# Transposing DMAs for seven heads' outputs and ScalarE's own x*sigmoid(x) in the first layer of a two-layer trunk

## The reference, cut to what matters

```python
proj = x @ w_in
xm, z, o_pre = proj[..., :E], proj[..., E:2 * E], proj[..., 2 * E:3 * E]      # E = 2048, 8 heads of 256
xc = jax.nn.silu(_causal_dwconv(xm, conv_w, conv_b))                          # 4 taps
q, k = xc @ w_q * DK ** -0.5, xc @ w_k                                        # by head
v = xm @ w_v
h = _mlstm_chunkwise(q, k, v, i_pre, log_sigmoid(f_pre))                      # 8 chunks of 128 tokens
hn = (h - mean(h)) * rsqrt(var(h) + eps) * norm_g                             # over a head's 256 channels
hb = sigmoid(o_pre) * hn + skip * xc
branch = (hb * jax.nn.silu(z)) @ w_out
x = layer_norm(alpha * x + branch)
```

## Time and profile before

| what | value |
|---|---|
| median of 3 runs (lowest to highest) | 1388.66 us (1387.12 to 1392.43) |
| the profiled execution: its time, its span | 1388.29 us, 1386.5 us |
| TensorE busy | 1374.8 us, 99% of the span |
| VectorE busy | 1155.4 us, 83% |
| ScalarE busy | 754.4 us, 54% |
| GpSimd busy | 147.5 us, 11% |
| chain that ended last | TensorE 94%, VectorE 3%, ScalarE 1% |

### The profile page before, as it was taken

The page is one execution under the profiler, slowest core; times in us unless marked ns, Lnnn a source line. Parts: engine busy times, 40 slices in busy tenths (PEclk is TensorE's granted clock), DMA queues, the critical chain, the costliest instruction groups (busy, mean ns, idle before and its releaser), DMA issues.

```text
span 1386.5 us, 19098 instructions
## 1 busy us (share of the span) xinstructions
PE 1374.8 (99%) x6602; PEld 1150.8 (83%) x6602; DVE 1155.4 (83%) x1891; ACT 754.4 (54%) x1318; POOL 147.5 (11%) x246
## 2 busy tenths in 40 slices
PE   9999999999999999999999999999999999999997
PEld 7888888888888888888888888888888888888886
DVE  6989899898998989899874446797888888889976
ACT  5775766657576674757733436564333333336340
POOL 1001011010201101010000001001111111100021
PEclk9999999999999999999999999999999999999999
DMA  6115344262534426245497767434666555699651
GB/s 235 49 39 145 97 123 112 72 182 54 140 96 118 118 76 172 65 137 180 138 334 244 221 190 226 129 118 112 168 159 165 156 135 157 180 298 324 215 198 76
DMA packets 103809, 213.44 MB, mean 154 GB/s; under 512 B 11010, under 2 KB 27906, under 8 KB 102562
## 3 DMA queue, kind: packets, MB, share of 16 engines
q1 hardware_dynamic: 90914, 178.66, 38.7%
q0 software_dynamic: 12800, 33.56, 13.0%
HBM read 170.11 MB, written 75.63 MB: 177 GB/s over the span
## 4 chain that ended last, share of the span: by engine, by line
PE 94%; DVE 3%; ACT 1%; DMA 1%; issue 1%; POOL 0%; DVEq 0%; SPq 0%; ACTq 0%; POOLq 0%
PE wide L2935 20%; PE wide L2937 20%; PE wide L2936 20%; PE ps_state L2935 3%; PE ps_state L2937 3%; PE ps_state L2936 3%; PE ps_inter L2936 2%; PE ps_inter L2935 2%; PE ps_inter L2937 2%; PE ps_intra L3114 2%; PE ps_intra L2937 2%; PE ps_intra L2935 2%; PE ps_s L2935 2%; PE ps_s L2936 2%; PE ps_s L2937 2%; PE ps_intra L2936 2%
## 5 line engine op out<-in xcount | busy, mean ns | idle before, releaser
L2936 PE MATMUL wide<-xa,inb 128*128 128x512 f32 x576 | 224.7, 390 | 0.0
L2935 PE MATMUL wide<-xb,inb 128*128 128x512 f32 x472 | 189.5, 402 | 0.7 <-DVE inb L1941 0.5
L2937 PE MATMUL wide<-xb,inb 128*128 128x512 f32 x472 | 184.3, 391 | 0.0
L2936 PEld LDWEIGHTS wide<-xa,inb 128*128 128x128 f32 x576 | 108.4, 188 | 20.2
L2936 PE MATMUL wide<-xa,blk 128*128 128x512 f32 x320 | 124.5, 389 | 0.0
L2937 PEld LDWEIGHTS wide<-xb,inb 128*128 128x128 f32 x472 | 88.6, 188 | 19.2
L2935 PEld LDWEIGHTS wide<-xb,inb 128*128 128x128 f32 x472 | 88.8, 188 | 18.5 <-issue 0.8
L2935 PE MATMUL wide<-xb,blk 128*128 128x512 f32 x256 | 99.7, 389 | 0.0
L2937 PE MATMUL wide<-xb,blk 128*128 128x512 f32 x256 | 99.6, 389 | 0.0
L1860 ACT ACTIVATE wy<-wy_raw 128x1024 fp32r<-128x1024 f32 x56 | 59.4, 1062 | 61.0 <-DMA wy_raw<-y_block 60.7
L2935 PE MATMUL wide<-xa,inb 128*128 128x512 f32 x208 | 83.2, 400 | 0.7 <-DVE inb L1941 0.7
(11 more groups left out here) (439 smaller groups left out, 3951.3 us busy)
## 6 DMA issues: line engine op xcount, KB each, us to landing
in_raw<-in_w_in SPq DMA_DIRECT2D x45, 512.0 KB, 4.2
wy_raw<-y_block SPq DMA_DIRECT2D x56, 256.0 KB, 4.2
mw_raw<-h_block SPq DMA_DIRECT2D x53, 256.0 KB, 3.3
m_sum<-in_w_out POOLq DMA_DIRECT2D x48, 256.0 KB, 4.3
h_block<-f_buf SPq DMA_DIRECT2D x48, 256.0 KB, 3.5
w_sum<-in_pool_w_out POOLq DMA_DIRECT2D x48, 256.0 KB, 4.3
a_raw<-in_pool_w_z SPq DMA_DIRECT2D x16, 512.0 KB, 3.7
a_raw<-folded SPq DMA_DIRECT2D x16, 512.0 KB, 4.6
```

What stands on the lines that cost most here:

```text
L2935: pe.matmul(dst, a[0], b[0], start=first, stop=False, skip_group_check=more)
L2936: pe.matmul(dst, a[0], b[1], start=False, stop=False, skip_group_check=more)
L2937: return pe.matmul(dst, a[1], b[0], start=False, stop=last, skip_group_check=more)
```

## The change

The outputs of heads 0 to 6 are no longer turned by TensorE (`turn_head` is gone; the last head's `turn` stays). In its place, for each half f of a head's chunks: `part_turn` (ScalarE, two copies 128x1024) takes the float32 numbers apart into their two 16-bit halves in `apart`; `move_turned` (SyncE) turns each of the two with a DMA transpose, 128 by 8 blocks of 128; `join_turn` (ScalarE, two copies) joins the halves again in `joined`, from which `y_turned` reads. On all eight heads the activation function Silu takes the place of tanh and VectorE's product: `silu_z` and `silu_conv` write in place, `gate_out_z` and `gate_conv` are gone, and the factors that undid the missing halves are dropped in `scale_columns`. Silu lies in another activation table than Exp and Tanh, so a table is loaded before the first `silu_z` and again by the preload of Exp. The queues are written in another order around this.

```diff
+            def move_turned(h, f):
+
+                sp.wait_ge(h_apart, 2 * h + f + 1)
+                if f:
+                    sp.wait_ge(h_moved, 64 * h + 32)
+                for part in range(2):
+                    sp.dma_start_transpose(turned_at(f, part), apart[:, f, part, :]).then_inc(h_moved, 16)
...
             for h in range(1, HEADS):
                 load_in(3 * h + 1, 0)
                 load_in(3 * h + 1, 1)
+                move_turned(h - 1, 0)
                 load_qkv(h)
                 load_in(3 * h + 2, 0)
                 load_rows(h)
-                store_h(h - 1, 1, 2)
+                move_turned(h - 1, 1)
                 load_in(3 * h + 2, 1)
-                store_h(h - 1, 5, 3, 7)
+                store_h(h - 1, 1, 2, 5, 3, 7)
...
+            def silu_z(h, n):
+
+                ready, (j, m) = ((in_c11, (0, 0)), (in_c22, (1, 1)), (in_c21, (1, 0)), (in_c12, (0, 1)))[n]
+                act.wait_ge(ready, 3 * h + 2)
+                act.activation(z_buf[:, j, half(m)], z_buf[:, j, half(m)], ACT.Silu).then_inc(z_made[n // 2], 1)
...
-            def tanh_conv(h, j):
+            def silu_conv(h, j):
                 act.wait_ge(conv_ready, 2 * h + 2 - j)
+                act.activation(xc_at(h, j), xc_at(h, j), ACT.Silu).then_inc(xc_ready, 1)
...
+            def part_turn(h, f, part):
+
+                act.wait_ge(hn_ready, 2 * h + f + 1)
+                act.wait_ge(s_full, NC * (h + 1))
+                ins = act.activation(apart[:, f, part, :].rearrange("p (c d) -> p c d", d=DV),
+                                     num[:, 4 * f:4 * f + 4, 0:DV].bitcast(U16).rearrange("p c (d b) -> p c d b", b=2)[:, :, :, part], ACT.Copy)
+                if part:
+                    ins.then_inc(h_apart, 1)
+
+            def join_turn(h, f, part):
+
+                act.wait_ge(h_moved, 64 * h + 32 * (f + 1))
+                ins = act.activation(joined[:, f, :, :].bitcast(U16).rearrange("p j (c t b) -> p c j t b", t=P, b=2)[:, :, :, :, part],
+                                     turned_at(f, part).rearrange("p (c j) t -> p c j t", j=2), ACT.Copy)
+                if part:
+                    ins.then_inc(turn_full, 2)
...
             def y_turned(h, m, b=None):
...
-                turned = (ps_inter, ps_s)[m % 2][:, :] if b is None else b
+                turned = joined[:, n, j, :] if b is None else b
...
@@ second_half, ScalarE
                 in_snapshot(3 * h + 1, 6)
+                join_turn(h - 1, 0, 0)
+                join_turn(h - 1, 0, 1)
                 in_upper_right(3 * h)
                 in_snapshot(3 * h + 1, 5)
+                join_turn(h - 1, 1, 0)
+                join_turn(h - 1, 1, 1)
                 in_high(x + 16)
                 in_high(x + 17)
+                high_qkv(h)
...
@@ second_half, VectorE
                 tap(h, 1, 2)
                 tap(h, 1, 3)
+                y_turned(h - 1, 0)
+                in_join(3 * h + 1, 5)
+                y_turned(h - 1, 1)
                 in_sum(3 * h + 2, 0)
-                y_turned(h - 1, 3)
-                in_join(3 * h + 1, 5)
                 in_low(x + 16)
                 in_low(x + 17)
                 in_sum(3 * h + 2, 1)
                 in_sum(3 * h + 2, 2)
+                y_turned(h - 1, 2)
+                y_finish(h - 1, 0)
+                y_turned(h - 1, 3)
+                in_join(3 * h + 1, 4)
+                y_finish(h - 1, 1)
+                y_finish(h - 1, 2)
+                in_low(x + 18)
                 h_difference(h - 1, 5)
+                in_sum(3 * h + 2, 3)
                 y_finish(h - 1, 3)
...
@@ the products of the first layer, TensorE
-                if h:
-                    if (kind, q) == (X_OF, 5):
-                        turn_head(h - 1, 0)
-                    elif (kind, q) == (Z_OF, 1):
-                        turn_head(h - 1, 1)
-                    elif (kind, q) == (Z_OF, 6):
-                        turn_head(h - 1, 2)
-                    elif (kind, q) == (Z_OF, 7):
-                        turn_head(h - 1, 3)
```

More of the change, by code:

```diff
@@ L334, in build @@
                 xm_hi = sA("xm_hi", [P, 2, S], F32R, whole)
+            with ExitStack() as whole:
+                apart = sA("apart", [P, 2, 2, S], U16, whole)
+            with ExitStack() as whole:
+                joined = sA("joined", [P, 2, 2, HALF], F32, whole)
             qT = sA("qT", [P, S])
@@ L1287, in high_xm @@
                 act.wait_ge(conv_ready, 2 * h + 2)
-                if h == 0:
+                if h:
+                    act.wait_ge(turn_taken, 4 * h)
+                else:
                     act.wait_ge(rows_full, 1)
@@ L1363, in group_hi @@
                 else:
-                    act.wait_ge(wg_in, 16 * (g + 1))
+                    act.wait_ge(wg_in, WG_IN + 16 * (g + 1))
                 raw, hi, _ = group_part(g, m)
@@ L1379, in abs_log_gates @@
                 assert n[0] == ACT_LN
-                act.preload_act_table(ACT.Tanh)
+                act.preload_act_table(ACT.Exp)
             def gate_weights():
@@ L1434, in first_half @@
                 take_num(h - 1, 6)
+                part_turn(h - 1, 0, 0)
+                part_turn(h - 1, 0, 1)
                 take_num(h - 1, 7)
@@ L1437, in first_half @@
                 in_high(x + 11)
-                in_high(x + 12)
                 in_snapshot(3 * h + 1, 1)
                 first_tap(h, 1)
+                in_high(x + 12)
+                norm_head(h - 1, 1)
+                part_turn(h - 1, 1, 0)
+                part_turn(h - 1, 1, 1)
                 in_high(x + 13)
-                high_qkv(h)
-                norm_head(h - 1, 1)
                 in_high(x + 14)
@@ L1472, in second_half @@
                 skip_term(h, 0)
+                silu_z(h, 3)
+                act.preload_act_table(ACT.Exp)
             def next_head(h):
@@ L1620, in _ @@
             in_snapshot(2, 1)
-            tanh_z(0, 0)
+            silu_z(0, 0)
             in_high(11)
             in_high(12)
-            tanh_conv(0, 1)
-            tanh_z(0, 1)
-            tanh_conv(0, 0)
+            silu_conv(0, 1)
+            silu_z(0, 1)
+            silu_conv(0, 0)
+            silu_z(0, 2)
+            in_copy(1, 0, 1)
+            silu_z(0, 3)
             in_high(13)
+            act.preload_act_table(ACT.Exp)
             high_xm(0, 0)
@@ L1978, in in_join @@
                 dve.tensor_tensor(dst, wide[:, at, :], dst, op).then_inc(done, 1)
-            def gate_out_z(h, n):
-                j, m = ((0, 0), (1, 1), (1, 0), (0, 1))[n]
-                dve.wait_ge(z_tanh, 4 * h + n + 1)
-                t = o_buf[:, 0, half(1)] if n % 2 else z_gate[:, :]
-                dve.scalar_tensor_tensor(out=z_buf[:, j, half(m)], in0=t, scalar=1.0, in1=z_buf[:, j, half(m)],
-                                         op0=ALU.add, op1=ALU.mult).then_inc(z_gated, 1)
             def tap(h, j, i):
@@ L2302, in next_head @@
                 in_join(3 * h + 2, 2)
-                gate_out_z(h, 0)
                 low_v(h, 0)
@@ L2307, in next_head @@
                 in_low(x + 22)
-                gate_out_z(h, 1)
                 in_low(x + 23)
@@ L2330, in first_layer_out @@
                 in_join(PAIRS_A - 1, 2)
-                gate_out_z(last, 0)
                 in_join(PAIRS_A - 1, 5)
@@ L2341, in first_layer_out @@
                 low_k(last, 0)
-                gate_out_z(last, 1)
                 low_v(last, 2)
@@ L2348, in first_layer_out @@
                 low_k(last, 1)
-                gate_out_z(last, 2)
                 unit_lo(0)
                 y_factor_o(last, 0)
-                gate_out_z(last, 3)
                 low_k(last, 2)
@@ L2478, in _ @@
             gate_columns()
-            gate_conv(0, 1)
-            gate_conv(0, 0)
             low_xm(0, 0)
-            gate_out_z(0, 0)
             low_xm(0, 1)
@@ L2492, in _ @@
             in_low(15)
-            gate_out_z(0, 1)
             weighted_q(0)
```

104 lines of the change are left out of this document (35 added, 69 removed).

## The result

The changed kernel takes 1407.66 us (median of 4 runs, 1404.05 to 1409.62) beside 1388.23 us of the kernel before on the same chip: a ratio of 1.0134, 95% interval 1.0112 to 1.0156. It is 19.4 us slower where 7.0 were forecast. The sign was right and the time lies in the range, but the loss is almost three times the forecast one. The profiled execution took 1406.16 us, its span is 1404.4 us (before 1386.5).

The account below looks back on a forecast made before the run. TensorE, busy 99%, bounds the kernel, with VectorE's stretch before low_qkv the narrow place. Per head -1.88 + 2.2 + 0.7 = +1.0 us, seven heads +7.0, gives 1395.7 us; range 1380 to 1414.

Parts of the forecast that it names:

- The saving: On TensorE, four turns a head removed in seven heads: 1.88 us a head, 13.2 us in all.
- 19.3 us: VectorE's stretch from in_join(Z_OF, 5) to low_qkv, counted by instructions; TensorE leaves 18.14 us for it.
- 0.55 lost: In that stretch VectorE waits 0.55 us at in_low(x + 16) for ScalarE, whose second join_turn pair goes first.
- 0.45: At the stretch's end high_xm waits for the last tap, so low_xm starts at 312.5, not 312.05.
- The copy's bound from above (2.08): Rival at join_turn: strided copies take 2.08 us per 1024 columns, 16 us in all, 1412 us.
- A head has lost 2.2: At values, low_qkv ends 2.2 us behind TensorE in each head, against 1.88 won.
- Another 0.7 us: At k, behind values: ScalarE's queue with the second table load makes low_v late, 0.7 us a head.
- Head 0 ... no change over 1 us: Head 0 and the last head trade VectorE's products for two table loads, with no change over 1 us.
- The table load: On ScalarE, two a head at 1.28 us each, nothing beyond; the first covered, the second not.
- transposes that land late: Rival at join_turn: transposes later than 6.9 us delay values, 1410 to 1437 us; eight blocks in series, near 1560.
- late or slow copies: Case at join_turn: transposes or copies late by a few microseconds, up to 1414 us, chance 0.15; far later 0.08.
- The full gain: Rival: VectorE passes the stretch before low_qkv in 18.1 us, TensorE never waits, 1375.5 us, chance 0.15.

Follow-up runs that it names:

- the experiment with 64 columns: The changed kernel with y_finish of heads 0 to 6 on 64 of its 512 columns: 1396.29 us, ratio 1.0068 to the kernel before.
- the first experiment: The changed kernel with head 0's ScalarE order edited so a snapshot stands ahead of the last Silu and table load: 1403.21 us, ratio 1.0113 to the kernel before.

## Why the prediction was wrong

**The saving** (1.88 us a head) was right: 1.92 measured, 13.4 in seven heads.

**"19.3 us" for the stretch, "0.55 lost" and "0.45"** is the step that failed first, and it cost most. The mechanism was the right one, and the stretch; the sum of 20.3 was 21.5 in the trace. Most entries were a little low: ScalarE's copies start every 1.22 us and not every 0.95, which makes the wait 0.92 and not 0.55; a `y_turned` every 0.66 us and not 0.60 (three of them, 0.2); the pair of `h_difference` 1.34 and not 1.20; a wait of 0.18 ahead of an `in_sum`; 0.53 at `high_xm` for 0.45. The copy's bound from above (2.08) had been written down as a rival and the nearest row taken, and it lay between. Each 0.1 us in this stretch is a whole 0.1 of each head, since the slack was gone: 20.3 gave a stall of 2.2, 21.5 gives 3.3. (A slip on the way did no harm: between the start of `in_low(x + 16)` and the end of the last tap lie eighteen instructions and three taps, not nineteen; the 311.45 goes by eighteen.)

**"A head has lost 2.2"** had a second, smaller gap: the price of waiting itself. In three heads TensorE ran at the lower clock for 3.4 to 3.8 us behind the wait, and their `values` part is 20.4 to 20.5 and not 19.8. Two stretches of the changed kernel (us, busy and instructions of PE, PEld, DVE, ACT, POOL, granted clock, DMA share, GB/s), the head with the lower clock and the head shown above:

```profile
234.00:238.00 4.00, 3.42 (x8) 2.65 (x9) 3.96 (x5) 1.27 (x3) 0.19 (x1) 0.60 0.92 280
318.30:322.30 4.00, 3.96 (x17) 3.30 (x18) 3.68 (x4) 1.43 (x3) 0.55 (x1) 1.00 0.95 313
```

The 0.6 to 0.7 us are less than they look, because those heads wait no longer at `values` and hardly at k: from first product to first product they take 84.0 us in the mean, and the other four 83.7.

**"Another 0.7 us" at k** was too much in the mean: 0.38, and in three heads 0.1 or nothing. TensorE comes to k later than forecast by what it lost at `values`. One delay hid part of the other, as the experiment with 64 columns shows from the other side.

**"Head 0 ... no change over 1 us"** was wrong by 4.06 us in the profiled execution. The products and loads there were called a trade without reading head 0's queue: a Silu and a table load stand ahead of a snapshot that TensorE needs, and the wait of 2.61 brought six matmuls at a pitch of 0.43 and not 0.23 us with it, 1.2 us more. That second part comes and goes with the clock, as the first experiment says.

**The table load** was rightly put at 1.28 us with nothing beyond it: the activation behind the load at 66.52 starts at 67.81, and the removal of all 16 new ones gives 4 to 5 us. The Trainium skill, in "ScalarE: Activation LUTs", What ACT_TABLE_LOAD costs, has another 1380 ns for each; no load of this trace shows them (0.02 us lie before each and 0.01 behind it), and the trace decides. Which of the two loads of a head matters was also right: the one behind the last tap (without both, k falls by 0.32 us a head and `values` by 0.07).

**The transposes** landed in 3.1 to 6.3 us. A head's second pair was down 4.5 to 6.6 us behind its first issue, within the budget of 6.9 that was given it; ScalarE never waited for one. The 1309 ns for each block in "VectorE: DVE Perf Modes", The three transpose paths, of the Trainium skill do not add up over the eight blocks of one DMA here, and that rival falls with "transposes that land late". The copies with a stride, the other half of that rival, came out at 1.36 us, between the value taken and the rival's 2.08. The time, 1407.66, lies above the forecast's own 1390 to 1402, in the band given to late or slow copies (up to 1414); that is in part luck, as the copies have only 1 to 5 us of it.

**"The full gain"** did not come for this order. Its bound of 18.1 us for the stretch is a right one, but only where the join also starts on time, and an order that comes near to both has the sign turned.

The sum again with what was measured: seven heads of -1.92, +3.62 and +0.38 are +14.5, head 0 is +4.06, the rest of the program -0.7. Against the forecast the stall at `values` missed by 1.4 us a head, 9.9 in all (1.2 of the 1.4 are the longer stretch, the rest mostly the lower clock), head 0 by 4.1, and k by 2.2 the other way.

## What to carry to other kernels

Where a nearly full engine feeds one without slack, read the instructions that frame its narrow stretch, add every entry at its measured pitch in that place and every wait, compare with the time the other engine leaves, and expect the sum to be low. Look at the start of the stretch as well: what is moved ahead of its first instruction can make that one late. Work taken off that engine elsewhere is worth nothing there (4.7 us a head here). Before giving such a change up, move out of the stretch what need not be in it: the same operations took 1407.7 us in one order and 1379.2 in another.

## What was not expected of the hardware

- A ScalarE copy of 1024 16-bit columns takes 1.05 us written side by side, and 1.36 written to every second column in alternating blocks; reading every second one (`part_turn`) takes 1.05.
- SyncE is held for 1.32 us by the issue of each transposing DMA, against 0.33 (median; 1.08 at most) for an `in_raw` load, and once for 3.31.
- Behind a wait of 2.0 to 2.6 us TensorE's granted clock was full in some heads and 0.57 to 0.67 over the next 4 us in others, in which it then started matmuls every 0.43 us and not every 0.23. In head 0 the same wait of 2.6 us, with the same instructions before it, was followed by a full clock in one kernel and by the lower one in two. No run here tells which it will be.
